# Softmax sums of 29 attention blocks: inverted once in eight columns, moved by transfers

## The reference

```python
p = jax.nn.softmax(logits, axis=-1)                                   # sparse
return jnp.einsum('bhqk,bqkd->bqhd', p.astype(v.dtype), vg)
...
e = jnp.exp(logits - m)                                               # local
p = e / (jnp.sum(e, axis=-1, keepdims=True) + jnp.exp(sink - m))
o = jnp.einsum('bnhgqk,bnkhd->bnqhgd', p.astype(v.dtype), vb)
```

## Time and profile before

| What | us |
|---|---|
| median of 3 runs | 3504.48 (3496.69 to 3513.81) |
| the profiled execution, its own time | 3499.58 |
| its span, first to last instruction | 3497.8 |
| mean granted TensorE clock | 0.973 of full |
| PE busy | 3282.8 |
| DVE busy | 2577.1 |

### The profile page before, as it was taken

One profiled execution on the slowest core, in us unless ns is written; L12 is line 12 of the kernel. 1 busy time (PEld: TensorE's weight loads), 2 busy tenths in 40 slices (PEclk: granted clock), 3 DMA queues, 4 the chain that ended last, 5 costly groups with the idle time before them and its releaser, 6 DMA issues.

```text
span 3497.8 us, 40660 instructions
## 1 busy us (share of the span) xinstructions
PE 3282.8 (94%) x14500; PEld 2605.2 (74%) x14552; DVE 2577.1 (74%) x3844; ACT 1659.1 (47%) x2222; POOL 992.8 (28%) x592
## 2 busy tenths in 40 slices
PE   7999999987889998998988899999899999999998
PEld 5788778865566665667876687788788887888887
DVE  5899999957777767446646599999899999443444
ACT  5669887124555665673212243444544444312211
POOL 1012232343555666660020144332133231000000
PEclk9999999997999999999999999999999999999999
DMA  6323233542221111026565423232322222623422
GB/s 171 55 85 97 88 113 98 170 141 53 63 59 44 49 51 31 14 78 211 172 204 188 114 97 132 97 104 83 118 87 73 91 94 98 222 94 123 168 97 93
DMA packets 243524, 368.97 MB, mean 105 GB/s; under 512 B 45309, under 2 KB 152461, under 8 KB 235518
## 3 DMA queue, kind: packets, MB, share of 16 engines
q1 hardware_dynamic: 242270, 362.01, 33.3%
q0 software_dynamic: 1056, 4.36, 0.3%
HBM read 268.63 MB, written 97.68 MB: 105 GB/s over the span
## 4 chain that ended last, share of the span: by engine, by line
PE 40%; DVE 23%; issue 6%; ACT 5%; DMA 2%; SPq 1%; POOL 1%; DVEq 0%; ACTq 0%; POOLq 0%
PE rs_ps L88 8%; PE rs_ps L89 8%; PE rs_ps L90 8%; DVE m_ul L1595 4%; DVE m_cval L1648 2%; PE rs_ps L1946 2%; PE rs_ps L1973 2%; PE rs_ps L1947 2%; PE rs_ps L1902 2%; PE rs_ps L1975 2%; PE rs_ps L1974 2%; DVE m_cg L1647 1%; DVE m_cval L1647 1%; ACT m_cg L1334 1%; DVE den L1523 1%
## 5 line engine op out<-in xcount | busy, mean ns | idle before, releaser
L88 PE MATMUL rs_ps<-m_xh,m_uh 128*128 128x512 f32 x1344 | 529.2, 394 | 10.9 <-DVE m_u L1621 5.7
L90 PE MATMUL rs_ps<-m_xh,m_ul 128*128 128x512 f32 x1344 | 526.2, 392 | 0.0
L89 PE MATMUL rs_ps<-m_xl,m_uh 128*128 128x512 f32 x1344 | 526.1, 391 | 0.0
L1108 POOL TENSOR_TENSOR plo<-pf,phi 128x1024 fp32r<-128x1024 f32 x168 | 401.8, 2393 | 324.7 <-ACT phi L1210 321.6
L88 PE MATMUL frt_acc<-frt_xh,frt_wh 128*128 128x512 f32 x864 | 338.5, 392 | 11.0 <-issue 6.6
L89 PE MATMUL frt_acc<-frt_xl,frt_wh 128*128 128x512 f32 x864 | 338.5, 392 | 0.0
L90 PE MATMUL frt_acc<-frt_xh,frt_wl 128*128 128x512 f32 x864 | 338.5, 392 | 0.0
L88 PEld LDWEIGHTS rs_ps<-m_xh,m_uh 128*128 128x128 f32 x1344 | 254.6, 189 | 68.5 <-DVE m_ul L1595 11.8
L88 PE MATMUL rs_ps<-m_wh,m_hh 128*128 128x512 f32 x768 | 299.6, 390 | 4.6 <-DVE m_u L1636 4.5
L1208 ACT ACTIVATE pf<-rs_ps 128x1024 f32<-128x1024 f32 x168 | 172.0, 1024 | 271.1 <-PE rs_ps L1949 144.7
L89 PE MATMUL rs_ps<-m_wlo,m_hh 128*128 128x512 f32 x768 | 299.5, 390 | 0.0
(11 more groups left out here) (287 smaller groups left out, 7702.8 us busy)
## 6 DMA issues: line engine op xcount, KB each, us to landing
m_ur<-in_w_up_dram SPq DMA_DIRECT2D x48, 1024.0 KB, 5.7
m_wr<-in_w_down_dram SPq DMA_DIRECT2D x60, 512.0 KB, 4.5
zt<-frt_out SPq DMA_DIRECT2D x108, 256.0 KB, 4.7
frt_wr<-in_w_main_dram SPq DMA_DIRECT2D x51, 512.0 KB, 4.3
ht<-m_cg SPq DMA_DIRECT2D x48, 512.0 KB, 3.0
m_hr<-ht SPq DMA_DIRECT2D x96, 256.0 KB, 3.0
m_raw<-zt SPq DMA_DIRECT2D x64, 256.0 KB, 4.1
m_sg<-zt SPq DMA_DIRECT2D x64, 256.0 KB, 4.8
```

Of the source, the lines that this page charges most:

```text
L88: pe.matmul(out, ahi, bhi, start=first, stop=False)
L89: pe.matmul(out, ahi, blo, start=False, stop=False)
L90: return pe.matmul(out, alo, bhi, start=False, stop=last)
L1108: pool.tensor_tensor(plo[:, k % PS, :], pf[:, k % PS, :], f32(phi[:, k % PS, :]), ALU.subtract).then_inc(S["pl"], 1)
```

## The change

For blocks 0 to 28 (`by_row` = 29), the sums take another way. ACT and DVE each evict one row of sums of 512 columns (rows 64 and 96 of `ov`) in place of two copies of 64x256. SP moves the two rows by DMA into `rc8`, 128 partitions by 8 columns (`move_sums`, at `finish`). DVE inverts those 8 columns in one instruction, one tick after the finish. SP stores them to `dn` in DRAM, waits until they have landed, and loads them back, each row spread over 64 partitions, into `den` (`spread_inverses`, at `invert`). The scaling stands three ticks after the finish and waits for both loads. Mask loads from n = 5 on no longer stand with the queries: SP issues them, in the order of the plan, once it is past the logits that they wait for. Blocks 29 to 31 stay as they were.

```diff
@@ the plan
+        by_row = len(seq) - 3
...
-                    if b < len(seq) - 3:
-                        later += done
-                    elif b == len(seq) - 3:
-                        later += done[:2]
+                    if b < by_row:
+                        later += [(tick + 1, ("invert", b, 0)), (tick + 3, ("scale", b, 0))]
+                    elif b == by_row:
+                        later += [(tick, op) for op in done[:2]]
                         held = done[2:]
...
-            plan += later[:2]
-            later = later[2:]
+            due = [e for e in later if e[0] <= tick][:2]
+            plan += [op for _, op in due]
+            later = [e for e in later if e not in due]
@@ SyncE
-                if not kind and n >= 2:
-                    if n >= 5:
-                        sp.wait_ge(S["std"], first[index[0, n - 3] + 1])
-                    sp.dma_start(msk[:, n % 3, 0:(n + 1) * P], mask[n, :, 0:(n + 1) * P]).then_inc(S[f"lm{n % 3}"], 16)
+                if not kind and 2 <= n < 5:
+                    load_mask(n)
+
+            def load_mask(n):
+                if n >= 5:
+                    sp.wait_ge(S["std"], first[index[0, n - 3] + 1])
+                sp.dma_start(msk[:, n % 3, 0:(n + 1) * P], mask[n, :, 0:(n + 1) * P]).then_inc(S[f"lm{n % 3}"], 16)
...
+            def move_sums(b):
+                sp.wait_ge(S["eva"], b + 1)
+                sp.dma_start(rc8[0:DH, b % 2, :], den[DH:DH + 1, b % 2].rearrange("p a q -> p (a q)")).then_inc(S["sm"], 16)
+                sp.wait_ge(S["evd"], b + 1)
+                sp.dma_start(rc8[DH:P, b % 2, :], den[P - 32:P - 31, b % 2].rearrange("p a q -> p (a q)")).then_inc(S["sm"], 16)
+
+            def spread_inverses(b):
+                sp.wait_ge(S["rc"], b + 1)
+                sp.dma_start(dn[b].rearrange("(p c) -> p c", p=P), rc8[:, b % 2, :]).then_inc(S["iv"], 16)
+                sp.wait_ge(S["iv"], 16 * (b + 1))
+                for e in range(2):
+                    sp.dma_start(den[e * DH:(e + 1) * DH, b % 2],
+                                 dn[b:b + 1].rearrange("o (a e q) -> o a e q", a=4, e=2)[:, :, e, :].broadcast_to([DH, 4, P])).then_inc(S["dd"], 16)
...
+            masks, begun = [], 0
             for op, b, x in plan:
+                while masks and begun >= first[index[0, masks[0] - 3] + 1]:
+                    load_mask(masks.pop(0))
                 if op == "q" and b + 2 < len(seq):
                     load_queries(b + 2)
+                    if seq[b + 2][0] == 0 and seq[b + 2][1] >= 5:
+                        masks.append(seq[b + 2][1])
+                elif op == "logits":
+                    begun = first[b] + x + 1
...
+                elif op == "finish" and b < by_row:
+                    move_sums(b)
+                elif op == "invert" and b < by_row:
+                    spread_inverses(b)
@@ GpSimd, scale
-                pool.wait_ge(S["rc"], 4 * (b + 1))
+                if b < by_row:
+                    pool.wait_ge(S["dd"], 32 * (b + 1))
+                else:
+                    pool.wait_ge(S["rc"], by_row + 4 * (b - by_row + 1))
@@ ScalarE, evict
+                if b < by_row:
+                    act.activation(den[DH:DH + 1, b % 2].rearrange("p a q -> p (a q)"), ov[DH:DH + 1, 0:CH], ACT.Copy)
                 for e in range(2):
                     rows = slice(e * DH, (e + 1) * DH)
-                    act.activation(den[rows, b % 2, 0:2], oe[DH:P, :, e, :], ACT.Copy)
+                    if b >= by_row:
+                        act.activation(den[rows, b % 2, 0:2], oe[DH:P, :, e, :], ACT.Copy)
                     last = act.activation(y[rows, b % 2, 0:2], oe[0:DH, :, e, :], ACT.Copy)
@@ VectorE, evict
+                if b < by_row:
+                    dve.tensor_copy(den[P - 32:P - 31, b % 2].rearrange("p a q -> p (a q)"), ov[P - 32:P - 31, CH:QW])
                 for e in range(2):
                     rows = slice(e * DH, (e + 1) * DH)
-                    dve.tensor_copy(den[rows, b % 2, 2:4], oe[DH:P, :, e, :])
+                    if b >= by_row:
+                        dve.tensor_copy(den[rows, b % 2, 2:4], oe[DH:P, :, e, :])
@@ VectorE, invert
+                if b < by_row:
+                    dve.wait_ge(S["sm"], 32 * (b + 1))
+                    dve.reciprocal(rc8[:, b % 2, :], rc8[:, b % 2, :]).then_inc(S["rc"], 1)
+                    return
@@ new tensors
+    dn = nc.dram_tensor("dn", (2 * NB, QW), F32).ap()
...
+                ("mm8", 161.25, [P, 2, HEADS], F32), ("rc8", 161.375, [P, 2, HEADS], F32), ("snk", 161.5, [P, HEADS], F32),
```

More of the change, by code:

```diff
@@ L594, with stage_rest @@
 ORDER = "0 w 1 w 2 w 3 w 4 w 5 w 6 w 7 w 8 w 9 w 10 w 11 w 12 w 13 14 w 15 w w"
-def stage_rest(nc, zt, mask, sinks, yt, ident, near, nearq, kva, pf, plo, phi, own, y, den, M,
+def stage_rest(nc, zt, mask, sinks, yt, dn, ident, near, nearq, kva, pf, plo, phi, own, y, den, M,
                x_in, w_pa, w_pb, w_o, ln1_g, ln1_b, x1, xs, ht, w_up, conv_w, conv_b, w_down, ln2_g, ln2_b, out):
@@ L611, in stage_rest @@
         bhi, blo, bq, msk, cm, cms = (M[n] for n in ("bhi", "blo", "bq", "msk", "cm", "cms"))
-        idb, idr, irep, junk, mx, mm8, snk = (M[n] for n in ("idb", "idr", "irep", "junk", "mx", "mm8", "snk"))
+        idb, idr, irep, junk, mx, mm8, rc8, snk = (M[n] for n in ("idb", "idr", "irep", "junk", "mx", "mm8", "rc8", "snk"))
         ps = s.ps("ps", [P, 8, CH])
@@ L619, in stage_rest @@
                  "lq0", "lq1", "lm0", "lm1", "lm2", "lb0", "lb1", "qr", "qd", "kh", "kd", "vt", "vh", "vd", "sqd", "sqr", "dvl",
-                 "mmd", "nm", "q2d", "std", "ex", "ph", "pl", "pv", "eva", "evd", "rc", "yd", "st0", "st1")
+                 "mmd", "nm", "q2d", "std", "ex", "ph", "pl", "pv", "eva", "evd", "rc", "yd", "st0", "st1", "sm", "iv", "dd")
         S = {n: s.sem(f"a_{n}") for n in names}
@@ L773, in stage_rest @@
                 plan += room[1:]
-            plan += later[:2]
-            later = later[2:]
+            due = [e for e in later if e[0] <= tick][:2]
+            plan += [op for _, op in due]
+            later = [e for e in later if e not in due]
             tick += 1
-        plan += later
+        plan += [op for _, op in later]
         users, where = [], {}
@@ L2170, in build @@
                 ("junk", 159, [P, 2, CH], BF16), ("mx", 161, [P, 2, HEADS, NCH], F32),
-                ("mm8", 161.25, [P, 2, HEADS], F32), ("snk", 161.5, [P, HEADS], F32),
+                ("mm8", 161.25, [P, 2, HEADS], F32), ("rc8", 161.375, [P, 2, HEADS], F32), ("snk", 161.5, [P, HEADS], F32),
                 ("khh", 161.75, [P, SEQ], F32R), ("klo", 169.75, [P, SEQ], F32R), ("vhi", 177.75, [P, NB, P], F32R),
@@ L2209, in build @@
                 stage_front(nc, xt, w_idx, w_main, rel_bias, onehot, zt, mask, bands, ident, sca, khh, near, nearq, kva)
-                stage_rest(nc, zt, mask, attn_sinks[0], yt, ident, near, nearq, kva, pf, plo, phi, own, y, den, M,
+                stage_rest(nc, zt, mask, attn_sinks[0], yt, dn, ident, near, nearq, kva, pf, plo, phi, own, y, den, M,
                            x[0], w_pa[0], w_pb[0], w_o[0], ln1_g, ln1_b, x1, xs, ht, w_up[0], conv_w[0], conv_b[0], w_down[0], ln2_g, ln2_b, out[0])
```

## The result

The changed kernel takes 3464.7 us (median of 4 runs, 3459.7 to 3466.9), the kernel before, beside it, 3507.4 us (4 runs); the ratio is 0.989, 95% interval 0.986 to 0.991. That is 42.6 us off by the medians.

What follows compares the result with a forecast made beforehand. PE bounds the kernel, standing in the attention for DVE, held by reciprocals. 35 + 2 + 5 - 7 - 1 = 34 us off 3499.6 gives 3465.6; with 4.9 for the median, 3470, range 3452 to 3486, chance 0.60.

Steps and rivals of the forecast that it cites:

- Reciprocals, 35 us: Attention: taking the 128x128 reciprocals off DVE saves 35 us, the middle between 28 and 43.
- Clock, 5 us: Attention: fewer PE stalls give back a fifth of the lost clock, 5 us, ends 0 and 10.
- What was late next: Attention, once the reciprocals leave DVE: PE itself is the next thing late.
- the 10 that I gave as a sign: Attention: PE's waits for maxima (L1489 and L1477) fall from 30.6 us to under 10.
- Eviction, 2 us: ACT's and DVE's copies of sums become one-row copies, 0.15 us less on each engine; gain 1 to 4, taken as 2.
- DVE's wait for sums, 7 us on the path: DVE stands up to 1.4 us a block until sums land; a third charged, 7 us, ends 0 and 41.
- POOL, 1 us, SP, 0: POOL waits up to 0.5 us at the scaling, charged 1 us; SP's extra issues and waits are free.
- The trip: Sums' way by DMA to the inversion and back: 8.8 to 13 us, against 12.5 us of cover.
- The slower rival: Return trip comes out at POOL, holding up plo and values: 38 us slower, 3542; chance 0.09.
- The second rival: DVE's wait for sums takes the reciprocals' place and PE sees it all: 2 us off, 3502; chance 0.16.
- The attention ends 34 us earlier: Sign: the attention part ends some 34 us earlier than before.
- All behind unchanged: Sign: everything behind the attention moves earlier with it, unchanged.

Runs made afterwards that it cites:

- e1: Kernel before with the four 128x128 reciprocals of blocks 0 to 28 replaced by one of 128x8, no transfers; 3463.9 us against 3508.6, ratio 0.988.
- e8: Changed kernel with the scaling in the same tick as the inversion; 3503.6 us in one execution against 3506.6 before, attention 749.6 us.
- e3: Kernel before with only the mask loads moved behind the logits; 3505.9 us against 3508.6, ratio 1.000.
- e6: Changed kernel with the old evictions, four copies of 64x256, in place of the one-row copies; attention 711.7 us in one execution.
- e4: Changed kernel with inversion two and scaling four ticks after the finish, semaphore split by parity; 3457.3 us against 3502.8 before, ratio 0.988.
- e9: The version of e4 again, on the same chip as the changed kernel; 3463.0 us against 3506.6 before, ratio 0.988.
- e5: Changed kernel with the scaling two ticks after the finish in place of three; attention 702.1 us.
- b0: The kernel before, run again unchanged; attention 752.0 us, 1948.6 us behind it.
- e7: Kernel before, all four 128x128 reciprocals kept but one a tick in four ticks, scaling with the last, no transfers; 3474.6 us against 3502.8, ratio 0.991.

## Why the prediction was right

The time was forecast at 3470 and came at 3465; 34 us off were forecast, 33.0 measured between the two profiled executions and 42.6 by the medians. The larger one is the fair one, since the profiled execution of before happened to be quick behind the attention. That 33.0 lies so near 34 is luck: it is 47.2 us off in the attention less 12.7 lost behind it. The forecast named the right place, the right sign and the right order of size; of its terms, those for standing come to 29 us net (35 + 2 - 7 - 1) against 28.2 measured, with parts that differ, and the clock's 5 against 19.0. Step by step:

- **Reciprocals, 35 us.** Right in kind, too large: by the table above e1 has 27 us less of such waits, apart from `m_klb` (38.1 to 11.3). Of the readings the 28 from the timeline (1.15 of 1.77) was the best, and the middle of 28 and 43 was no better than its ends.
- **Clock, 5 us.** Mis-sized, outside my 0 to 10: 19.0 us less busy time in the two profiles, 15 to 23 over the repeats of both kernels (685.0 and 682.0 against 666.0, 662.1 and 667.2). What failed is "most dips follow the longer stalls, which stay". The first 50 us stay low (0.82 and 0.84), but no load of keys or queries was taken away, and yet the mean granted clock of the attention rose from 0.96 to 0.98. It goes with the standing: e8, where PE stands 69.5 us again, has 0.96 and 680.0 us busy. A part differs from execution to execution, as e3 shows (0.97 and 677.0 us with all reciprocals in place, 0.95 in its first 300 us).
- **Not in the sum: 12 us** of `m_klb` beside POOL. The forecast had no term for it.
- **What was late next.** I named PE itself; the waits show it, with 11.3 us left for maxima, just over the 10 that I gave as a sign.
- **Eviction, 2 us.** The rows are 588 and 697 ns against 760 and 854, as estimated; the 6.0 us row for one partition was no guide. e6 puts it at 2 to 7. PE's waits for evictions grew all the same, from 7.0 to 10.1 us. The shorter copies aren't the cause: e1, with the old ones, has 9.6. That PE arrives earlier once the reciprocals are gone is my reading.
- **DVE's wait for sums, 7 us on the path.** It came, 28.2 us in all, near the 20 that I worked from, up to 5.3 us where window key loads stood ahead on SP. On PE it costs 7.3 us by the table, as forecast. e4 and e9 take it away and are no quicker in the attention, for `m_klb` takes 5.3 us back.
- **POOL, 1 us, SP, 0.** POOL's wait was 8.8 us. SP's own three largest that are tied to sums and scaling, from 790 to 1560 us:

```profile
SPq L929 <- ACT y L1256: 139.3, 21, 41.7
...
SPq L925 <- POOL y L1135: 119.6, 27, 11.1
...
SPq L938 <- DMA dn<-m_rc: 43.7, 29, 3.3
```

They total 302.6 us of 770, and none of PE's waits in the attention is for a DMA. They aren't free where DVE stands behind them, as at 885 us.
- **The trip.** Small transfers landed in 1.7 us, under both of my rows (2.3 and 3.7), the way back in 2.9. By its own terms the trip of the forecast sums to 9.4 to 13.5 us and not 8.8 to 13: the issue of the middle transfer was left out. The Trainium skill ("DMA: Bandwidth & Descriptors", Specifications) has transfers under 512 B read, modify and write. If that costs time here, it isn't enough to bring 4 KB in 32-byte pieces above 1.7 us, against 2.3 us for the 256 KB store; no run sends the same bytes in larger pieces, so its cost isn't shown.
- **The slower rival.** POOL's lateness can cost what the whole change gains, but neither the way nor the threshold was as written. e5 shows slack for one tick. e8, two ticks earlier, loses 40 to 45 us at a wait of 4.5 us a block (131.3 over 29; 14.2 in one), where the forecast had some 6 us of it free. The forecast had called SP's store of y free; here it stands ahead of the next sums. That is one part, the larger one is `m_klb`; late values have none. The changed kernel lies one tick on the safe side.
- **The second rival** (the wait takes the reciprocals' place) falls by the result itself, 3465 against its 3502.
- **The attention ends 34 us earlier:** 45.7. **All behind unchanged:** within what repeats differ (1948.6 in b0 against 1946.2 to 1951.5).

## What to carry to other kernels

A slow instruction on an engine that is not the bound costs what it adds behind the last thing that the bound waits for, and not its own duration: 107 us of reciprocals cost 27 us of waits and a share of the clock. Before building transfers to be rid of such work, place it one piece a tick: e7 got two thirds of the gain by a change of the plan and one semaphore more. With transfers, look at what stands behind each wait in the issuing queue: the changed kernel's return trip was free with its consumer two ticks behind the inversion and still free at one (e5), and dear at none (e8). Moving work of one engine also shifts what the others meet; here 12 of the 28 us less standing came from that, and 5 us of it hid a cost when e4 was tried. So before calling a wait free, look at what stands ahead of each wait of the bound engine. Where a change removes many short gaps, count the clock as well, here 19 of 47 us; and take two profiles of the kernel before ahead of a sum against one.

## What the runs showed of the hardware that I had not expected

- A tensor_tensor of 64x256 from SBUF to SBUF on VectorE takes 0.41 us, and up to 2.6 us beside an instruction of GpSimd; all 34 long ones of three profiles end 0.27 to 0.28 us after a GpSimd instruction.
- Small DMAs are quick: SBUF to SBUF from one row into 64 partitions (2 KB) and SBUF to DRAM in 32-byte pieces (4 KB) both land in 1.7 us from issue, median of 58 and 29.
- A copy of one partition by 512 columns from PSUM takes 697 ns on VectorE and 588 ns on ScalarE, less than two of 64 partitions by 256 columns (854 and 760), while one of 1x1024 from SBUF had taken 6.0 us. That one, from 781.6 to 787.6 us, also lay beside GpSimd, which was busy from 778.5 to 787.7 with hardly a gap.
- One stretch of the MLP has two speeds in executions of the same kernel, at the same granted clock (0.98): 1027 or 970 weight loads in 240 us. The slower ones have short waits of PE's weight loads for DVE (0.8 us at most, 8.9 to 11.0 us in total), the quicker ones none from 2240 us on. Of the 14 profiles two are quick, before's and e7's (1938.8 and 1940.0 us behind the attention; the other 12 took 1946 to 1953). What starts it was not looked for.
